# A decoder layer on one core: the mixer's heads written out, convolution taps spread over the units, samples as one block

## What is computed

```python
u = _rmsnorm(x, norm_mix) * (1 + sc2) + sh2
p = u @ w_in + b_in
ca, cg, q, k, v, o, ga, gb, ip, fp = _split_cols(p)
glu = ca * jax.nn.sigmoid(cg)
y, conv_new = _causal_dwconv(glu, conv_buf, w_dw, b_dw)       # 31 taps, depthwise
a_out = jax.nn.silu(_layernorm(y, ln_conv_g, ln_conv_b)) @ w_conv_out
hm, C, n, m = _mlstm_chunkwise(heads(q), heads(k), heads(v), ip, jax.nn.log_sigmoid(fp), C0, n0, m0, chunk)
hm = _headnorm(hm, mh_norm).reshape(Bn, T, D_MLSTM).astype(x.dtype)
b_out = (jax.nn.sigmoid(o) * hm) @ w_mlstm_out
z = jax.nn.sigmoid(ga) * a_out + jax.nn.sigmoid(gb) * b_out
x = x + g2 * (z @ w_out)
```

## Time and profile before

| | us |
|---|---|
| median of 3 runs | 3418.8 (3417.13 to 3423.22) |
| span of the profiled execution | 3417.0 |
| PE busy | 3167.0 (93%) |
| DVE busy | 1597.9 (47%) |
| POOL busy | 1020.0 (30%) |
| ACT busy | 465.6 (14%) |

### The profile page before, as it was taken

How to read it: one execution, slowest core, us unless ns; L and a number is a source line. 1 busy time by engine, 2 the same in 40 slices (tenths; PEclk the granted TensorE clock), 3 DMA queues, 4 the chain that set the end, 5 groups by cost and what they waited for, 6 DMA issues and landing times.

```text
span 3417.0 us, 47244 instructions
## 1 busy us (share of the span) xinstructions
PE 3167.0 (93%) x18860; PEld 3029.7 (89%) x18860; DVE 1597.9 (47%) x2811; ACT 465.6 (14%) x746; POOL 1020.0 (30%) x449
## 2 busy tenths in 40 slices
PE   8999999999968889879888997989998999999995
PEld 8999999999958778878787895789887999999995
DVE  5122233222276943973694397476344233232335
ACT  2000000000031122012112211322012000000001
POOL 1233333333312311321231142034332333333331
PEclk9999999999989999999999998999998999999997
DMA  6312121212121112212211221222210111111111
GB/s 221 106 62 74 61 74 61 74 61 68 49 75 41 44 42 68 70 34 60 74 50 42 68 70 51 60 103 93 108 50 25 44 44 44 47 43 43 43 43 59
DMA packets 83136, 217.63 MB, mean 64 GB/s; under 512 B 28352, under 2 KB 28480, under 8 KB 82496
## 3 DMA queue, kind: packets, MB, share of 16 engines
q1 hardware_dynamic: 83000, 215.86, 19.7%
q10 hardware_dynamic: 8, 0.00, 0.0%
HBM read 184.03 MB, written 31.81 MB: 63 GB/s over the span
## 4 chain that ended last, share of the span: by engine, by line
PE 73%; DVE 16%; issue 5%; DVEq 3%; POOL 1%; DMA 1%; ACT 1%; SPq 0%; ACTq 0%; POOLq 0%
PE slots L575 61%; DVE y L1072 12%; PE bank_x L637 3%; PE bank_x L758 2%; DVEq L1376 2%; PE bank_x L750 1%; PE bank_x L765 1%; PE bank_y L762 1%; PE bank_y L767 1%; DVE work L1100 1%; PE bank_y L637 1%; DMA w_raw<-w_units_dram 1%; PE bank_y L740 1%; PE bank_x L775 0%; PE bank_x L748 0%
## 5 line engine op out<-in xcount | busy, mean ns | idle before, releaser
L543 POOL TENSOR_TENSOR w_hi<-w_raw,one 128x1024 fp32r<-128x1024 f32 x220 | 437.9, 1990 | 2317.9 <-PE slots L575 2247.3
L575 PE MATMUL slots<-u_hi,w_hi 128*128 128x364 f32 (+1 forms) x4032 | 930.3, 339 | 53.0 <-DVE u_lo L1133 20.2
L575 PE MATMUL slots<-u_hi,w_lo 128*128 128x364 f32 (+1 forms) x4032 | 899.5, 332 | 0.0
L575 PE MATMUL slots<-u_lo,w_hi 128*128 128x364 f32 (+1 forms) x4032 | 898.4, 331 | 0.0
L575 PEld LDWEIGHTS slots<-u_hi,w_hi 128*128 128x128 f32 x4032 | 699.4, 191 | 81.4 <-issue 65.4
L575 PEld LDWEIGHTS slots<-u_hi,w_lo 128*128 128x128 f32 x4032 | 705.3, 190 | 9.2 <-issue 8.7
L575 PEld LDWEIGHTS slots<-u_lo,w_hi 128*128 128x128 f32 x4032 | 708.2, 191 | 0.0
L545 POOL TENSOR_TENSOR w_lo<-w_raw,w_hi 128x1024 fp32r<-128x1024 f32 x220 | 581.3, 2642 | 17.2
L1163 DVE TENSOR_TENSOR work<-work,slots 128x1092 f32<-128x1092 f32 x44 | 56.9, 1292 | 913.5 <-PE slots L575 913.5
L1072 DVE SCALAR_TENSOR_TENSOR y<-glu,dw_cur,y 128x1024 f32 (+1 forms) x240 | 344.7, 1436 | 9.1
L1072 DVE SCALAR_TENSOR_TENSOR x<-slots,m_g,x 128x728 f32<-128x728 f32 x368 | 257.8, 742 | 0.0
(11 more groups left out here) (219 smaller groups left out, 2187.4 us busy)
## 6 DMA issues: line engine op xcount, KB each, us to landing
w_raw<-w_units_dram SPq DMA_DIRECT2D x220, 512.0 KB, 3.6
ada<-ada_units_dram SPq DMA_DIRECT2D x72, 512.0 KB, 4.2
st<-state_dram SPq DMA_DIRECT2D x32, 257.0 KB, 3.7
C_s_out<-st SPq DMA_DIRECT2D x32, 257.0 KB, 3.6
x_keep<-x SPq DMA_DIRECT2D x1, 4368.0 KB, 12.7
ga_keep<-th SPq DMA_DIRECT2D x8, 546.0 KB, 5.6
gb_keep<-th SPq DMA_DIRECT2D x8, 546.0 KB, 5.6
th<-gb_keep SPq DMA_DIRECT2D x8, 546.0 KB, 4.6
```

The source lines that it names most:

```text
L543: pool.tensor_tensor(w_hi[:, slot, :], w_raw[:, slot, :], one[:].to_broadcast([P, D]), ALU.mult).then_inc(w_hi_done, 1)
L575: last = pe.matmul(slots[:, s, g, 0:b - a], w_of(w), r[:, k, a:b], start=(k == 0 and q == 0), stop=(k == K - 1 and q == 2))
```

## The change

- The heads are no longer a loop. `UNITS` lists all 64 units of the mixer in order; each head has 15 (q, k, v, o, then three merge units and four convolution units; the last head has seven merge units), so that the merge units of all heads stand among chunk steps. The units' place in memory is unchanged; `stored` finds it.
- The pieces have fixed places (`HEAD_PLAN`: unit of the head, k-tile behind which the piece stands). S: scores of four chunks into one bank, then of all samples as one block of 64. T: k and v of a chunk (or of all samples) to token order. N: numerator and denominator of a chunk, added up in one bank. M: the same for the samples, four at a time, from `qz`, q spread to blocks of 64 columns with zeros. U and X: memory of a chunk and of a sample, both halves in one DVE instruction over two banks. B: outputs back to feature order, two chunks at a time.
- The decay weights of a head come from one broadcast: DVE lays the row's values on diagonals (`spread_diagonals`), PE multiplies them by a constant matrix (`spread_rows`), ACT makes the inter-chunk weight and the exponentials (`decay_weights`), DVE adds the masks (`masked_rows`). q is multiplied by the inter-chunk weight once per head, in place.
- The taps are spread over the first eleven units of a head (`TAPS`); in DVE's queue one stands behind each piece, the rest at the unit's end.
- The inverse root is made twice per head for all chunks at once. The row work before the first head is cut in parts with the first evacuations between them.
- Sample states have four buffers; SP loads the first four in units 0 to 3 and the others in unit 11 of a head.

```diff
--- before.py
+++ after.py
...
+            out = [("gate", 0), ("value", 0), ("gate", 1), ("value", 1)]
+            merge = [(half, k) for half in ("b", "a") for k in range(KT)]
+            for h in range(H):
+                out += [("q", h, 0), ("q", h, 1), ("k", h, 0), ("k", h, 1), ("v", h, 0), ("v", h, 1), ("o", h, 0), ("o", h, 1)]
+                if h < H - 1:
+                    out += [("merge", 3 * h + n, *merge[3 * h + n]) for n in range(3)]
+                    out += [(what, 2 * h + 2 + t) for t in range(2) for what in ("gate", "value")]
+                else:
+                    out += [("merge", 3 * h + n, *merge[3 * h + n]) for n in range(7)]
...
+        HEAD_PLAN = {
+            4: [(4, "S", 0), (5, "S", 1)],
+            5: [(1, "S", 2)],
+            6: [(2, "T", NC), (5, "T", 0)],
+            7: [(1, "N", 0), (4, "U", 0), (6, "T", 1)],
+            8: [(0, "N", 1), (2, "U", 1), (4, "M", 0), (7, "T", 2)],
+            9: [(0, "N", 2), (2, "U", 2), (3, "X", 0), (5, "X", 1), (7, "T", 3)],
+            10: [(0, "N", 3), (2, "U", 3), (3, "X", 2), (5, "X", 3), (7, "T", 4)],
+            11: [(0, "N", 4), (2, "U", 4), (7, "T", 5)],
+            12: [(0, "N", 5), (2, "U", 5), (3, "M", 1), (5, "B", 0), (7, "T", 6)],
+            13: [(0, "N", 6), (2, "U", 6), (3, "X", 4), (4, "X", 5), (5, "B", 2), (7, "T", 7)],
+            14: [(0, "N", 7), (2, "U", 7), (4, "X", 6), (6, "X", 7)],
+        }
+        LAST_PLAN = {0: [(2, "B", 4), (5, "B", 6)], 1: [(1, "B", NC)]}
+        TAPS = [[0, 3, 3, 3, 2, 2, 4, 4, 4, 3, 3], [3, 3, 3, 3, 2, 2, 3, 3, 3, 3, 3]]
...
+            def after(bank, n):
+                if bank != "y":
+                    pe.wait_ge(x_free, n["x"])
+                if bank != "x":
+                    pe.wait_ge(y_free, n["y"])
+                pe.wait_ge(p_free, n["p"])
+                n[bank] += 1
...
+            def spread_rows(h):
+                s = open_slot()
+                pe.wait_ge(diag_ready, h + 1)
+                for g in range(2):
+                    pe.matmul(slots[:, s, g, :], mean[:], dw[:, g * 512:(g + 1) * 512], start=True, stop=True)
+                pe.matmul(slots[:, s, 2, 0:SL], mean[0:SL, :], dw[0:SL, NP:NT], start=True, stop=True).then_inc(part_done, 1)
+                jobs.take_part()
...
+            def numerators(h, c):
+                a = c * CH
+                after("y", used)
+                pe.wait_ge(x_free, USE["T", h, c])
+                if c == 0:
+                    pe.wait_ge(x_free, USE["S", h, 2])
+                    pe.wait_ge(y_free, USE["S", h, 1])
+                    pe.wait_ge(qt_ready, h + 1)
+                else:
                     for m in range(2):
+                        pe.matmul(bank_y[:, 0:C1], q_of(m, a, CH), c_cur[:, m, :], start=(m == 0), stop=False)
+                pe.matmul(bank_y[:, 0:C1], dw[:, a:a + CH], kvt[:, c % 2, HD:2 * HD + 1], start=(c == 0), stop=True).then_inc(y_full, 1)
...
+            def memory(h, c):
+                after("p", used)
+                pe.wait_ge(vws_ready, h * 16 + VWS_AT["p", c])
+                pe.matmul(bank_x[:, 0:C1], kvt[:, c % 2, 0:P], vws[:, c % 2, :], start=True, stop=True)
+                pe.matmul(bank_y[:, 0:C1], kvt[:, c % 2, P:HD], vws[:, c % 2, :], start=True, stop=True).then_inc(p_full, 1)
...
+            def memory_sample(h, b):
+                after("p", used)
+                pe.wait_ge(vws_ready, h * 16 + VWS_AT["s", b])
+                pe.matmul(bank_x[:, 0:C1], kvs[0:SL, 0:P], vwss[0:SL, b % 2, :], start=True, stop=True)
+                pe.matmul(bank_y[:, 0:C1], kvs[0:SL, P:HD], vwss[0:SL, b % 2, :], start=True, stop=True).then_inc(p_full, 1)
...
+            def decay_weights(h):
+                s, done, freed = jobs.take_part()
+                act.wait_ge(part_done, done)
+                if h:
+                    act.wait_ge(b_out, 16 * h)
+                act.activation(qkvo[:, 6, 0:NT], slots[:, s].rearrange("p g n -> p (g n)")[:, 0:NT], ACT.Exp,
+                               scale=float(D)).then_inc(win_ready, 1)
...
+            def tap(h, j):
+                dve.drain()
+                if j == 0:
+                    dve.wait_ge(glus_in, 32 * (h + 1))
+                for t in range(2):
+                    k = 2 * h + t
+                    yt, w = y[:, k, :], w_dw[:, k, j:j + 1]
+                    for out, src in ((yt[:, 0:NP], glu[:, t, j:j + NP]),
+                                     (sample3(yt[:, NP:NT]), glus[:, t, :, j:j + TB])):
...
+            def spread_diagonals(h):
+                dve.drain()
+                dve.tensor_tensor(dw[:, 0:NP].rearrange("p (c l) -> p c l", c=NC), ident[:].unsqueeze(1).to_broadcast([P, NC, CH]),
+                                  col[:, :, 4 + h:5 + h].to_broadcast([P, NC, CH]), ALU.mult)
+                dve.tensor_scalar(dw[0:SL, NP:NT], ident[0:SL, 0:SL], cols[:, 4 + h:5 + h], None, ALU.mult).then_inc(diag_ready, 1)
+            def masked_rows(h):
+                s, _, _ = jobs.take_part()
+                dve.wait_ge(win_ready, h + 1)
+                stt(dw[:, 0:NP].rearrange("p (c l) -> p c l", c=NC), slots[:, s, 0:2, :].rearrange("p g (c l) -> p (g c) l", c=4),
+                    float(D), mask[:].unsqueeze(1).to_broadcast([P, NC, CH]), ALU.mult, ALU.add)
+                stt(dw[0:SL, NP:NT], slots[0:SL, s, 2, 0:SL], float(D), masks[:], ALU.mult, ALU.add).then_inc(slot_free[s], 1)
...
+                elif what == "N":
+                    dve.wait_ge(y_full, USE["N", h, c])
+                    a = c * CH
+                    stt(den[:, c:c + 1], bank_y[:, HD:C1], -1.0, col[:, c, 8 + h:9 + h], ALU.mult, ALU.max)
+                    dve.tensor_copy(qkvo[:, 4:6, a:a + CH], bank_y[:, 0:HD].rearrange("p (m n) -> p m n", m=2))
+                    dve.drain()
+                    dve.tensor_tensor(den[:, c:c + 1], bank_y[:, HD:C1], den[:, c:c + 1], ALU.max).then_inc(y_free, 1)
...
+                elif what == "U":
+                    dve.drain()
+                    dve.wait_ge(p_full, USE["U", h, c])
+                    if c == 0:
+                        if h:
+                            dve.wait_ge(c_out, 16 * h)
+                        dve.tensor_copy(c_cur[:], pair[:, :, 0:C1]).then_inc(p_free, 1)
+                    else:
+                        stt(c_cur[:], c_cur[:], ap_all[:, h, c:c + 1], pair[:, :, 0:C1], ALU.mult, ALU.add).then_inc(p_free, 1)
+                elif what == "X":
+                    dve.wait_ge(p_full, USE["X", h, c])
...
+            evacuate(0)
+            evacuate(1)
+            row_maxima()
+            evacuate(2)
+            evacuate(3)
+            row_differences()
+            for i in range(4, MIXER):
+                h, u = divmod(i - 4, UNITS_HEAD)
+                if u == 4:
+                    masked_rows(h)
+                if u == 11:
+                    inverse_denominators(0)
+                taps = list(range(taps_before(h, u), taps_before(h, u + 1)))
+                for _, what, hh, c in plan(i):
+                    piece(what, hh, c)
+                    if u == 14 and what == "N":
+                        inverse_denominators(1)
+                    if taps:
+                        tap(h, taps.pop(0))
+                for j in taps:
+                    tap(h, j)
+                if u == 3:
+                    spread_diagonals(h)
+                if u == 11:
+                    normalise(h, 0)
+                if u == 14:
+                    normalise(h, 1)
+                evacuate(i)
+            for i in range(MIXER, N_PLANNED):
...
-            def taps(h):
-                tiles = [2 * h, 2 * h + 1]
-                pick = lambda t: (y[:, tiles[t], :] if isinstance(h, int) else y[:, bass.ds(tiles[t], 1), :].rearrange("p a n -> p (a n)"))
-                if isinstance(h, int):
-                    dve.tensor_copy(dw_cur[:], w_dw[:, 2 * h:2 * h + 2, :])
-                else:
-                    dve.tensor_copy(dw_cur[:], w_dw[:, bass.ds(2 * h, 2), :])
-                for j in range(CW):
-                    if j == CW // 2:
-                        prelude(h)
-                    dve.drain()
...
```

More of the change, by code:

```diff
@@ L290, in sample3 @@
             return ap64.rearrange("p (b t) -> p b t", b=NB)
[L293 to L307, removed]
@@ L559, in _ @@
             hid = Tally()
-            xu, yu = Tally(), Tally()
-            steps, heads = Tally(), Tally()
-            sts = [Tally() for _ in range(3)]
             def open_slot():
@@ L768, in piece, with features_first @@
+            def features_first(h, c):
+                after("x", used)
+                pe.wait_ge(hs_ready, 9 * h + (c + 2 if c < NC else 9))
+                if c < NC:
+                    for m in range(2):
+                        for j in range(2):
+                            a = (c + j) * CH
+                            last = pe.transpose(bank_x[:, (2 * m + j) * P:(2 * m + j + 1) * P], qkvo[:, 4 + m, a:a + CH], ident[:])
                 else:
```

(36 more changed lines are left out.)

942 lines of the change are left out of this document (468 added, 474 removed).

## The result

The changed kernel takes 3227.98 us (median of four, 3224.19 to 3230.8) beside 3421.01 us for the kernel before on the same chip (3417.13 to 3424.47). The ratio is 0.9438, with an interval of 0.9425 to 0.945. The forecast was 3231, with a range of 3162 to 3303. The profiled execution spans 3225.0 us, the granted clock is 0.969 on the mean.

The account below looks back on a forecast made before the run. PE is the limit except where DVE's taps stand in its way. Start 1059, heads 249 + 3 x 246 and end 11 give 2057 against 2245, 188 us less: 3231 us, range 3162 to 3303.

Parts of the forecast that it names:

- changes between them: On PE, some 42 switches per head between projections and pieces, up to 0.1 us each, taken as 4 us a head.
- the walk: Step through heads 1 to 3: DVE's diagonals end near 60 us, PE is ready at 49, so it waits about 11.
- The state loads: Sample states loaded at the end of unit 11 for M1 in unit 12: 1.5 us of wait a head.
- 3.75 a pair: POOL's two split instructions of a weight unit stretch DVE's taps by 1.64 + 2.11 us.
- The extra time that the rule could have brought: Port lock holding DVE for a pair's whole time, up to 5.0 us: four pairs in four heads, up to 20 us longer.
- the slow stretch behind a wait: PE restarts slowly after a long wait: a unit takes 13.63 us instead of 12.0, so 1.6 added each.
- the start: Row work cut in two finds PE busy, so head 0 starts at 1059 us instead of 1071.
- its own case: The forecast's main case, chance 0.60, spanning 3200 to 3262 us with waits halved or doubled.
- the second rival: DVE late throughout units 7 to 10, 1.5 us at each of twelve pieces, 18 per head: 3303 us; chance 0.18.
- the first: Rival: taps are never late, removing 12.5 us from three heads and 15 from the first: 3178 us; chance 0.15.
- The third: Rival: slower than before, a tap ahead of each of 16 pieces, 3.75 us each: 3471 us; chance 0.05.
- no change: Rival: DVE still sets the head's length, needing 295 us of DVE work per head; chance 0.02.

Follow-up runs that it names:

- Experiment 3: Changed kernel with POOL splitting only 8 of 1024 columns in the mixer's 64 units, the rest of the split left out: 3148.44 us.
- Experiment 4: Changed kernel with each memory update of a sample (X) issued twice on PE: 3256.98 us.
- experiment 1: Changed kernel with `spread_diagonals` ahead of the first unit's taps in heads 1 to 3, not behind the fourth unit's: 3188.26 us.
- experiment 2: Changed kernel with four more taps ahead of the diagonals in heads 1 to 3 and four fewer behind them: 3260.37 us.
- experiment 9: Changed kernel with early diagonals and four more taps moved to the front, both in heads 1 to 3: 3231.41 us.
- experiment 8: Changed kernel with all row work (maxima and differences) again ahead of the first gate and value: 3237.76 us.
- experiment 5: Changed kernel with taps 1 to 29 of 31 left out: 3160.86 us.
- experiment 7: Changed kernel with early diagonals in heads 1 to 3, plus head 0's diagonals at unit 3's start and its taps respread: 3178.19 us.

## Why the prediction was right

**The limits and PE's share.** PE's price of a head was forecast as 15 x 12.0 + 46.6 for pieces + 4 for changes between them. Experiment 3 measures 226.4, and 180 + 46.6 is 226.6: the pieces were right as a sum, and the changes cost next to nothing, the lower of the two ends given. Experiment 4 shows that PE sets the pace among the X pieces.

**The waits.** At the broadcast 11 us were forecast for heads 1 to 3 and 10.8 came, each time; for head 0 it was 6 there and 5.5 at U1, and 7.5 and 5.5 came. Experiments 1, 2 and 9 show the cause as the walk had it: twelve taps and four pairs ahead of a service. The state loads were priced at 1.5 a head, and the seven waits sum to 3.1 over all heads.

**What POOL costs.** The row's 3.75 a pair is the price of a full meeting; the mean is 2.5, and DVE's busy time per head is 161 us beside 127 with POOL out of the way, where 138 and fifteen pairs at 3.75 would have been 194. The four pairs that decide, ahead of the diagonals, add 3.7 to 3.8 each in head 1, near the upper value, so the wait came out. The Trainium skill, SBUF — State Buffer, "SBUF: two separate sides", says that the one that starts second is blocked for the whole of the other's instruction. The trace agrees in kind: the first stretched tap, 0.28 long when alone, ends 0.09 us behind POOL's first instruction (1179.30 and 1179.21), and the second, 1.28 long, 1.09 behind POOL's second (1182.77 and 1181.68). The prediction had read the rows as if both ended with POOL's; the second waits and then does its work. The copies of N that read PSUM are not held: 20 of the 32 meet a split and take 0.41 to 0.42, like the other 12. The extra time that the rule could have brought, up to 20 us, did not come.

**Where terms were off and cancelled.** The changes (4 a head) and the state loads were too dear. Two were too cheap: the slow stretch behind a wait, 1.6 each and 8 in all in the forecast, took 17; and a wait at B in the first unit of heads 1 to 3, 1.9 each, had not been in the sum. The heads came to 980.6 us instead of 987, the end to 12.4 (2054.32 - 2041.92) instead of 11, the start to 1061.3 instead of 1059, and the whole to 2054.3 instead of 2057. In the heads, terms that were some 21 us too dear met others some 15 too cheap. The waits at the broadcast and at U1 were seen rightly; that the sum lies within 3 us of the measured time is partly luck.

Two numbers of the forecast don't come out of their own words. The waits and restarts of the sum are 63 us; half of them less gives the 3200 of its own case, but twice as much would be 3294 and not 3262. And half of the second rival with both last ones is 0.16, not 0.17. Neither decides anything here.

**The start.** Forecast as 12, it is 9.4 between the two profiles and 12 by experiment 8 for the head's start, 9.8 in the median. One profile can't give it more closely: in experiments 1, 2, 4, 5, 7 and 9 everything ahead of head 0 is as in the changed kernel, and there the head starts anywhere from 1059.3 to 1065.2.

**The rivals.** The taps are late, so the first is out, and what it was to give (heads near 231, 3178) is what experiments 1 and 7 reach by moving the diagonals. Units 7 to 10 are late only in head 0 (5.53 at U1 and 1.36 at X0; 0.5 at most in each other head), so the second is out. The third needed 2.9 us at each of 16 pieces, and "no change" an unchanged limit on DVE; neither shows in the waits.

## What to carry to other kernels

Where one engine's long work is spread out under another's, sum what stands in its queue ahead of each thing that the other one needs, and set that against the other's time to the same point: 161 us of DVE's work in a head of 245 still left 11 us of wait, because twelve taps and four disturbances stood ahead of one small instruction. Moving that one instruction ahead of the taps gave 40 us in three heads without a tap less; it had 2.3 us to spare at the next service, so look at that one before filling the room. And where a step is to be priced by taking it away, start from the row of the wait that it ends (80.9 here, 88 measured), not from the length of the stretch around it (115).

## What the runs showed of the hardware that was not expected

**The clock behind a wait.** In the changed kernel PE idles for 10.8 us ahead of the broadcasts of heads 1 to 3. The stretches behind it in heads 1 and 2, and last a stretch behind the wait of 1.98 us at B in head 2's first unit (granted clock third from the end):

```profile
1371.00:1374.00 3.00, 3.00 (x6) 1.02 (x5) 0.00 (x0) 0.17 (x1) 0.00 (x0) 0.58 0.00 0
1374.00:1384.00 10.00, 10.00 (x67) 10.00 (x67) 2.00 (x3) 3.61 (x10) 0.00 (x0) 1.00 0.01 2
...
1614.00:1617.00 3.00, 3.00 (x4) 1.09 (x4) 0.00 (x0) 0.00 (x0) 0.00 (x0) 0.50 0.00 0
1617.00:1627.00 10.00, 10.00 (x55) 9.25 (x55) 1.35 (x2) 3.77 (x10) 0.00 (x0) 0.89 0.00 0
...
1557.00:1562.00 5.00, 5.00 (x24) 5.00 (x23) 4.73 (x10) 0.00 (x0) 0.00 (x0) 0.66 0.97 261
```

The broadcast runs at half clock, the level of 1.2 GHz: 3.75 us for matmuls that take 1.88 in experiment 1, where no wait stands ahead of them:

```profile
1361.52 1.88 PE L817 MATMUL slots<-dw,mean 128*128 128x512 f32 x4
```

In head 1 the clock is back within the first stretch, in head 2 only in the second. PE's busy time above 226.4 is 2.8 us in head 1, and 4.7 and 4.9 in heads 2 and 3. The longer time at half clock behind the broadcast is the smaller part of that difference: PE works 4.0 us at half clock there in head 1 and 5.3 and 5.5 in the others, so some 0.7 us. The larger part stands behind the wait at B, where PE works another 3.4 us at half clock in heads 2 and 3, 1.7 us lost; in head 1 a like wait, 1.91 us, is followed by full clock. So like waits had unlike prices, and why is not shown here.

**Small instructions are held too.** At the end of the last head the normalisation works on five elements. DVE first, then POOL:

```profile
2041.28 0.17 DVE L1594 TENSOR_TENSOR small<-small 128x5 f32<-128x5 f32 x1
2041.52 0.17 DVE L1596 TENSOR_TENSOR small<-small 128x5 f32<-128x5 f32 x1
...
2042.01 1.83 DVE L1594 TENSOR_TENSOR small<-small 128x5 f32<-128x5 f32 x1
2043.91 2.35 DVE L1596 TENSOR_TENSOR small<-small 128x5 f32<-128x5 f32 x1
```

```profile
2041.92 1.89 POOL L619 TENSOR_TENSOR w_hi<-w_raw,one 128x1024 fp32r<-128x1024 f32 x1 [12.77 <-PE slots L646]
2043.89 2.35 POOL L621 TENSOR_TENSOR w_lo<-w_raw,w_hi 128x1024 fp32r<-128x1024 f32 x1
```

The same two instructions take 0.17 us alone and 1.83 and 2.35 beside a split, 3.84 more, within the 6.41 us that PE waits for the last B. The same hold stands at the start of heads 1 to 3 (L1596 takes 2.39 us at 1309.61): the waits of 1.9 us at B there are gone in experiment 3, with short splits, and stay in experiment 5, with few taps. A chain of tiny steps pays as much for one split as a stream of long taps.
